# Expert ring of a two-block kernel: slots that hold half the rows of both experts, an earlier conditional, and banks written twice

## The reference, cut to what matters

```python
def hierarchical_moe(h, w_rg, b_rg, w_re, b_re, w1, w3, w2):
    # top-1 of 4 groups, top-2 of the 8 experts in it; 32 experts, D=1024, D_EXPERT=512
    ...
    e_w = jax.nn.softmax(e_val, axis=-1) * g_w
    ...
    def expert_block(args):
        xb, e = args
        hid = jax.nn.silu(xb @ w1[e]) * (xb @ w3[e])
        return hid @ w2[e]
    ys = lax.map(expert_block, (xs, blk_expert)).reshape(n_pad, D)
    ys = ys * wpad[:, None].astype(ys.dtype)
    out = jnp.zeros((T + 1, D), ys.dtype).at[tok].add(ys)[:T]
```

## Time and profile before

| | |
|---|---|
| median of 3 runs | 1216.96 us (1216.36 to 1217.27) |
| profiled execution | 1213.47 us, span 1211.6 us |
| mean granted TensorE clock | 0.985 |
| PE busy | 1145.1 us, 95% of the span |
| DVE, ACT, POOL busy | 40%, 34%, 19% |
| queue of the weight loads | 330.36 MB, 70.0% of 16 engines' span |
| chain that ended last | PE 71%, DMA 20%, DVE 5%, issue 1% |
| of it, loads of expert weights | 18% (`DMA ring<-in_w`) |
| of it, expert products | 12% L1144, 4% L1185 |
| loads of expert weights | 91 of 2048 KB, 17.5 us median to landing |

### The profile page before, as it was taken

One profiled execution on the slowest core, in us unless ns is written; L12 is line 12 of the kernel. 1 busy time (PEld: TensorE's weight loads), 2 busy tenths in 40 slices (PEclk: granted clock), 3 DMA queues, 4 the chain that ended last, 5 costly groups with the idle time before them and its releaser, 6 DMA issues.

```text
span 1211.6 us, 15514 instructions
## 1 busy us (share of the span) xinstructions
PE 1145.1 (95%) x5898; PEld 764.6 (63%) x5898; DVE 488.0 (40%) x967; ACT 409.8 (34%) x607; POOL 231.8 (19%) x104
## 2 busy tenths in 40 slices
PE   4899999989999999999999997999999999999998
PEld 1578767774444444444444445878877777888886
DVE  1595552762222222222222214589544643323226
ACT  3533444231111111111111115654345354434334
POOL 0362233200000000000000001410312435342522
PEclk8899999989999999999999998999999999999999
DMA  9886466678889999999999995443313455554541
GB/s 378 335 305 242 146 229 251 277 279 341 352 341 423 422 422 422 422 422 421 422 421 422 421 421 207 144 153 138 123 71 125 162 185 163 184 164 175 207 157 52
DMA packets 89191, 331.64 MB, mean 274 GB/s; under 512 B 3873, under 2 KB 26690, under 8 KB 62514
## 3 DMA queue, kind: packets, MB, share of 16 engines
q1 hardware_dynamic: 88512, 330.36, 70.0%
q0 software_dynamic: 432, 0.48, 0.2%
q10 hardware_dynamic: 194, 0.06, 0.0%
HBM read 329.84 MB, written 1.05 MB: 273 GB/s over the span
## 4 chain that ended last, share of the span: by engine, by line
PE 71%; DMA 20%; DVE 5%; issue 1%; SPq 1%; ACT 1%; POOL 0%; DVEq 0%; ACTq 0%
DMA ring<-in_w 18%; PE ps L831 14%; PE ps L832 13%; PE ps L833 13%; PE ps L1144 12%; PE ps L1185 4%; DMA ring<-in_w_ada 2%; PE ps L891 1%; PE ps L1116 1%; PE ps L1117 1%; PE ps L1287 1%; SPq L716 1%; PE ps L945 1%; PE ps L943 1%; PE ps L882 1%
## 5 line engine op out<-in xcount | busy, mean ns | idle before, releaser
L806 POOL TENSOR_TENSOR ring_r<-ring,ring_r 128x1024 fp32r<-128x1024 f32 x80 | 207.6, 2615 | 825.5 <-ACT ring_r L1486 825.5
L1144 PE MATMUL ps<-ring,arena 128*64 128x512 f32 x1008 | 228.5, 599 | 17.5 <-DMA ring<-in_w 17.5
L832 PE MATMUL ps<-ring_r,hl_r 128*128 128x512 f32 x528 | 210.7, 399 | 0.0
L831 PE MATMUL ps<-ring_r,hl_r 128*128 128x512 f32 x480 | 196.5, 409 | 9.1 <-DVE ring_r L1908 5.1
L833 PE MATMUL ps<-ring_r,hr_r 128*128 128x512 f32 x480 | 191.6, 399 | 0.0
L1486 ACT ACTIVATE ring_r<-ring 128x2048 fp32r<-128x2048 f32 x90 | 167.2, 1906 | 62.6 <-PE ps L833 45.0
L1144 PEld LDWEIGHTS ps<-ring,arena 128*64 128x64 f32 x1008 | 72.7, 138 | 154.0 <-issue 151.5
L1908 DVE TENSOR_TENSOR ring_r<-ring,ring_r 128x2048 fp32r<-128x2048 f32 x50 | 118.3, 2373 | 92.8 <-ACT ring_r L1486 92.6
L831 PEld LDWEIGHTS ps<-ring_r,hl_r 128*128 128x128 f32 x480 | 91.5, 191 | 37.3 <-issue 14.7
L832 PEld LDWEIGHTS ps<-ring_r,hl_r 128*128 128x128 f32 x528 | 100.6, 191 | 22.0
L833 PEld LDWEIGHTS ps<-ring_r,hr_r 128*128 128x128 f32 x480 | 91.3, 190 | 22.3
(11 more groups left out here) (363 smaller groups left out, 1656.6 us busy)
## 6 DMA issues: line engine op xcount, KB each, us to landing
ring<-in_w SPq DMA_DIRECT2D x91, 2048.0 KB, 17.5
ring<-in_w_in SPq DMA_DIRECT2D x21, 2048.0 KB, 8.8
ring<-in_w_ada SPq DMA_DIRECT2D x8, 2048.0 KB, 8.6
ring<-in_w_ffn_gate SPq DMA_DIRECT2D x11, 1024.0 KB, 5.3
ring<-in_w_ffn_up SPq DMA_DIRECT2D x11, 1024.0 KB, 8.0
ring<-in_w_ffn_down SPq DMA_DIRECT2D x5, 2048.0 KB, 7.8
ring<-in_w_ada SPq DMA_DIRECT2D x8, 1024.0 KB, 9.3
ring<-in_w_o SPq DMA_DIRECT2D x2, 2048.0 KB, 7.7
```

Source lines behind the costliest of these rows:

```text
L806: nc.gpsimd.tensor_tensor(rest[:, a:b], w[:, a:b], lead[:, a:b].bitcast(F32), ALU.subtract).then_inc(sem("w_rest_b"), 1)
L831: mm(o, lhsT=a_lead, rhs=b_lead, start=start, stop=False, skip_group_check=True)
L832: mm(o, lhsT=a_lead, rhs=b_rest, start=False, stop=False, skip_group_check=True)
L1144: last = mm(H[slots_of(e), :], lhsT=xs[:, k, slots_of(e)], rhs=w, start=k == 0, stop=k == KD - 1)
```

## The change

A ring slot now holds one half h of the rows (of w1, w3 or w2) of both experts of a pair. The product of a half can run when its slot has landed, and the slot is free at its end. `moe_w1_used` and `moe_w3_used` count halves, and ScalarE's and VectorE's waits on them are doubled. In w2 the order of the matmuls is half of the rows first, column half second. SyncE waits slot by slot. The early w1 load takes half 0 of both experts instead of all of one. `keep_x` writes all four banks before the rank matmuls, two of them again, and the other two again behind the rank. TensorE's conditional stands ahead of the last four pairs; these turns are written in both of its branches.

```diff
+LATE_TURNS = 4
-        MOE_USED = ("w1_used", "w1_used", "w3_used", "w3_used", "ys1_done", "ys1_done")
+        MOE_USED = ("w1_used", "w1_used", "w3_used", "w3_used", "ys0_done", "ys1_done")
...
+        def block_used(n, pairs):
+            return sem("moe_" + MOE_USED[n]), 2 * pairs - 1 + n % 2 if n < 4 else pairs
...
-            w = expert_w[n][bass.ds(2 * pair + n % 2, 1)]
-            view = ring[:, MOE_SLOT[n], :]
-            src = w.rearrange("e (h p j) n -> p (e h) (j n)", p=P, j=2 if n >= 4 else 4)
-            view = view.rearrange("p (h r) -> p h r", h=2)
+            w = expert_w[n][bass.ds(2 * pair, 2)]
+            view = ring[:, MOE_SLOT[n], :].rearrange("p (e r) -> p e r", e=2)
+            src = w.rearrange("e (h p j) n -> h p e (j n)", p=P, j=2 if n >= 4 else 4)[n % 2]
...
-            src = expert_w[0][2].rearrange("(h p j) n -> h p (j n)", p=P, j=4)
-            for h in range(2):
-                sp_.dma_start(early_w1[h], src[h]).then_inc(sem("early_w1_in"), 16)
+            for e in range(2):
+                src = expert_w[0][2 + e].rearrange("(h p j) n -> h p (j n)", p=P, j=4)
+                sp_.dma_start(early_w1[e], src[0]).then_inc(sem("early_w1_in"), 16)
...
-            sp_.wait_ge(sem("moe_w1_used"), 1)
-            expert_load(sp_, 1, 1, chunk_in)
-            expert_load(sp_, 0, 2, chunk_in)
-            sp_.wait_ge(sem("moe_w3_used"), 1)
-            expert_load(sp_, 2, 1, chunk_in)
-            expert_load(sp_, 3, 1, chunk_in)
+            for n, pair in ((0, 2), (1, 1), (2, 1), (3, 1)):
+                sp_.wait_ge(*block_used(n, 1))
+                expert_load(sp_, n, pair, chunk_in)
...
             with sp_.Fori(3, PAIRS) as i:
-                for n, name in enumerate(MOE_USED):
-                    sp_.wait_ge(sem("moe_" + name), i)
+                for n in range(6):
+                    sp_.wait_ge(*block_used(n, i))
                     expert_load(sp_, n, i, chunk_in)
...
-            for n in range(3):
+                into = dense.bank(f"moe{n}") if again else dense.claim(pe, f"moe{n}")
+                mm(into, lhsT=ident, rhs=x[:, t, h * COL:(h + 1) * COL], start=True, stop=True)
+
+            for n in range(4):
                 keep_x(n)
+            keep_x(0, True)
+            keep_x(1, True)
             o = small.claim(pe, "rank")
...
-            keep_x(3)
+            keep_x(2, True)
+            keep_x(3, True)
...
+                for h in range(2):
+                    if beside and h == 0:
+                        pe.wait_ge(sem("early_w1_in"), 32)
+                    else:
+                        chunk_ready(2 * n + h, i, done)
+                    if n == 0:
+                        pe.wait_ge(sem(f"moe_xs{h}_ready"), 4 * i + 4 * done + 4)
+                    for k in range(4 * h, 4 * h + 4):
+                        for e in range(2):
...
+                            last = mm(H[slots_of(e), :], lhsT=xs[:, k, slots_of(e)], rhs=w, start=k == 0, stop=k == KD - 1)
+                    last.then_inc(sem(("moe_w1_used", "moe_w3_used")[n]), 1)
...
-                for half, Y in enumerate((HA, HB)):
-                    for f in range(FT):
-                        for e in range(2):
+                for h in range(2):
+                    if not early:
+                        chunk_ready(4 + h, i, done)
+                    for half, Y in enumerate((HA, HB)):
+                        for f in (2 * h, 2 * h + 1):
+                            for e in range(2):
...
+                        if h == 1:
+                            last.then_inc(sem(f"moe_ys{half}_done"), 1)
...
-            with pe.Fori(3, PAIRS - 1) as i:
+            with pe.Fori(3, PAIRS - LATE_TURNS) as i:
                 turn(i, 0, 0)
-            last_turn(PAIRS - 1, 0, 0)
+            def late_turns():
+                with pe.Fori(PAIRS - LATE_TURNS, PAIRS - 1) as i:
+                    turn(i, 0, 0)
+                last_turn(PAIRS - 1, 0, 0)
             with pe.If(more > 0):
+                late_turns()
                 pe.wait_ge(sem("moe_ys_scaled"), 2 * PAIRS)
...
+            with pe.Else():
+                late_turns()
```

More of the change, by code:

```diff
@@ L556, in two_blocks @@
             landed[slot] += 16 * (PAIRS - len(BESIDE.get(n, ())))
-            busy[slot] = sem("moe_" + name), PAIRS
+            busy[slot] = sem("moe_" + name), 2 * PAIRS - 1 + n % 2 if n < 4 else PAIRS
         def in_ring(n, i):
@@ L752, in _ @@
             for n in (1, 2, 3):
-                sp_.wait_ge(sem("moe_" + MOE_USED[n]), 2)
+                sp_.wait_ge(*block_used(n, 2))
                 expert_load(sp_, n, 2, chunk_in)
@@ L768, in _ @@
                     e = sp_.snap(i % PAIRS)
-                    for n, name in enumerate(MOE_USED):
-                        sp_.wait_ge(sem("moe_" + name), i + PAIRS)
+                    for n in range(6):
+                        sp_.wait_ge(*block_used(n, i + PAIRS))
                         expert_load(sp_, n, e, spare_in)
@@ L1129, in up @@
             def up(n, H, i, done, beside=False):
[L1131 to L1145 removed]
+                for h in range(2):
[7 more added lines that the diff above has]
+                        for e in range(2):
+                            if beside and h == 0:
+                                w = early_w1[e][:, k * COL:(k + 1) * COL]
+                            else:
+                                w = wide(MOE_SLOT[2 * n + h])[:, 4 * e + k % 4, :]
+                            last = mm(H[slots_of(e), :], lhsT=xs[:, k, slots_of(e)], rhs=w, start=k == 0, stop=k == KD - 1)
+                    last.then_inc(sem(("moe_w1_used", "moe_w3_used")[n]), 1)
             def places(i, done, col0):
@@ L1159, in w2_rows @@
                     return early_w2[2 * e + f // 2][:, at % (2 * D):at % (2 * D) + COL]
-                return ring[:, MOE_SLOT[4 + e], at:at + COL]
+                at = (2 * e + f % 2) * D + half * COL
+                return ring[:, MOE_SLOT[4 + f // 2], at:at + COL]
             def middle(i, done, col0, more_pairs, early=0):
@@ L1177, in middle @@
                     pe.wait_ge(sem("early_w2_in"), 64 * early)
-                else:
-                    for e in range(2):
-                        chunk_ready(4 + e, i, done)
                 pe.wait_ge(sem("moe_hidT_ready"), i + done + 1)
-                for half, Y in enumerate((HA, HB)):
-                    for f in range(FT):
-                        for e in range(2):
-                            last = mm(Y[slots_of(e), :], lhsT=hidT[:, f, slots_of(e)],
-                                      rhs=w2_rows(e, f, half, early),
-                                      start=f == 0, stop=f == FT - 1)
-                    last.then_inc(sem(f"moe_ys{half}_done"), 1)
+                for h in range(2):
[4 more added lines that the diff above has]
+                            for e in range(2):
+                                last = mm(Y[slots_of(e), :], lhsT=hidT[:, f, slots_of(e)],
+                                          rhs=w2_rows(e, f, half, early),
+                                          start=f == 0, stop=f == FT - 1)
+                        if h == 1:
+                            last.then_inc(sem(f"moe_ys{half}_done"), 1)
             def combine(i, done):
```

26 lines of the change are left out of this document (5 added, 21 removed).

## The result

The changed kernel takes 1205.72 us (1203.98 to 1207.34) where the kernel before takes 1217.10. The ratio on record is 0.9912, 95% interval 0.9897 to 0.9927; the quotient of the two medians is 0.9907. Timed again on another chip it was 1206.88 against 1216.79, 0.9915 (0.9895 to 0.9936). The gain in the median is 9.9 to 11.4 us; 12.9 was predicted. The profiled execution took 1205.15 us, span 1203.3, and lies 8.3 us under the one of before (1213.47), which was itself 3.6 us under its median. Where these 3.6 us lie no trace shows, so what follows explains the 8.3.

The account below looks back on a forecast made before the run. The full queue of expert loads at 422 GB/s bounds the kernel. Earlier landing 6.7 + tail 7.0 - jump 0.8 = 12.9 us: profiled 1213.47 to 1200.6, median 1204.1; forecast's own range 1200 to 1208, with rivals (a), (b) 1198.5 to 1210.5.

Parts of the forecast that it names:

- Copies: Routing: six copies of x keep TensorE's clock up, so the first up projection ends 5.1 us earlier.
- rival (a): Routing: the clock still falls or the copies come too late; the 5.1 us go, 1209 us; chance 0.12.
- Slots at the front: Expert load queue: half-row slots fill holes, worth 1.6 to 2 us; with the copies, last landing 6.7 us earlier.
- The four holes that were left in the queue: Expert load queue: times still short of 422 GB/s at early w1, early w2, pair 3's first slot and its w2.
- Slots at the tail: Behind the last expert landing: only 3.5 us of w2 matmuls follow, so the last combine comes 3.0 us earlier.
- Conditional: Tail: jump moved ahead of pair 12; fq starts 12.0 us behind the landing, tail 7.0 us shorter, 3.0 from slots.
- The stall where it went: Jump at pair 12: TensorE 7.7 us late, 6.9 regained in later turns, 0.8 us left over.
- rival (b): New tail: clock falls in 2.5 us idle ahead of fq, costing 1.7 to 3.4 us, 1206 to 1207.5; chance 0.10.
- (c): Late loop: instructions missed again at two back edges and the exit, 16.5 us left over, 1220 us; chance 0.04.
- (d): Expert loads lose rate, stepping 2 MB between experts; slower than before, 1237 us at 387 GB/s; chance 0.05.
- (e): Expert load queue: holes stay and only the tail is gained, 6.2 us, 1211 us; chance 0.05.

Follow-up runs that it names:

- after2: The changed kernel, unchanged, timed and profiled again on another chip: 1206.88 us, ratio 0.9915 to the kernel before.
- after: The changed kernel itself, against the kernel before, in its first timing and profile: 1205.72 us, ratio 0.9912.
- u_cond: The changed kernel with TensorE's conditional put back behind the last pair: 1208.69 us, ratio 0.9941 to the kernel before.
- u_ring: The kernel before with the new copies of x and the early conditional, but without the half-row slots: 1210.39 us, ratio 0.9952 to the kernel before.
- empty_queue: The changed kernel with TensorE waiting for its own combine of pair 11 before the jump, so no matmul is queued: 1207.43 us, ratio 0.9920.
- warm_both_late2: The changed kernel with unused fill products in the last turn and ahead of fq and fk0, and two late turns instead of four: 1202.65 us, ratio 0.9886.
- fill_fk: The changed kernel with four unused 512-column products into fk0's free bank while TensorE waits for fk's weights: 1204.58 us, ratio 0.9895.
- warm_tail: The changed kernel with unused products filling TensorE's idle stretches in the last turn and ahead of fq: 1204.20 us, ratio 0.9889.
- late2: The changed kernel with two late turns instead of four, the jump standing ahead of pair 14: 1203.56 us, ratio 0.9888.
- nobranch: The changed kernel without TensorE's conditional and the further rounds, which this input doesn't take: 1202.21 us, ratio 0.9872.
- keep4: The changed kernel with four copies of x ahead of the rank matmuls instead of six, two again behind: 1204.12 us, ratio 0.9885.
- warm_both: The changed kernel with unused fill products in the last turn, ahead of fq and, four of them, ahead of fk0: 1201.20 us, ratio 0.9875.

## Why the prediction was right, and where not

The sign and the size came out: 9.9 to 11.4 us in the median instead of 12.9, within the forecast's own range. That the median came so close is partly luck: the sum was worked out on the profiled execution, and there the gain is 8.3. By its steps:

- **Copies: right, with a hole.** The front was to be 5.1 us earlier by them. Without a fall ahead of them it is 4.9 (after2: 20.0 to 15.1 behind the choice), in after's own execution 3.2 (20.0 to 16.9). The step that failed there is "six copies end at 261.1, so they are covered": it took 0.86 us a copy for granted. At 1.2 GHz they end at 264.2 and hold the rank matmuls up by 2.4 us, of which 1.7 are left at the end of the first w1 product. The text gave the price if the cover were gone, and rival (a) names copies that come too late, but neither says when that would be.
- **Slots at the front: right.** Predicted, with the copies, 6.7 us at the last landing. Measured 5.4 in after and 7.1 in after2; 5.9 to 7.1 in the seven others that have the slots and six copies and no fall inside the gather. The four holes that were left in the queue were forecast at 3.0, 1.2, 6.4 and 2.6 us and are 3.0, 1.5, 6.7 and 2.5 in after2. What was off is the split: the forecast gave the slots 1.6 by themselves and the clock 5.1, and alone they give 1.3 and 3.6; the rest comes only with both.
- **Slots at the tail: right.** 3.0 predicted, 3.2 measured (u_cond) and 3.0 (15.24 in u_ring to 12.2).
- **Conditional: right in sum.** The tail was to shrink by 7.0 and does by 7.5 where the clock held in the last w2 and TensorE wasn't late for it (12.2), 6.3 in after. What is late next was named rightly, ScalarE's split of fq and then the rows.
- **The stall where it went: over-priced.** The term was 5.24 + 2.5 us late at pair 12, 6.9 regained, 0.8 left. It is 1.83 late, and nothing is left in after's profile. The failed step is to move the 5.24 from a place with an empty queue to one with a full one. (The terms regained add up to 7.0, not 6.9.) Where TensorE was late by more, in empty_queue and warm_both_late2, 1.2 and 0.5 us are left at fq, so setting lateness against slack, as the forecast did, was right in kind.
- **The clock behind the tail: missed in the sum.** It was rival (b), at 1.7 to 3.4 us, with a chance of 0.10. It happened, 1.2 us in w2 and 1.6 in fq, and once more where it wasn't looked for, 1.1 at fk; 0.85 us went at the load of wo's weights, for which no cause is shown. That is 4.8 us in after, 3.6 of them behind fq's start. The rival was under-weighted though its own numbers had it: 2.5 us of idle were forecast ahead of fq, 2.34 came, and the earlier trace rows show a fall behind 3.4 us of idle, with light matmuls round it. Adding up: 12.9 + 0.5 (tail) + 0.8 (jump) + 0.3 (ahead of the choice) - 1.3 (front) - 4.8 = 8.4, where the two profiled spans differ by 8.3.

Rivals (c), (d) and (e) are out: one "issue" gap, 422 GB/s, and holes filled. Of (a) the clock in the gather held in after and after2 and fell in fill_fk; the late copies came in after.

**Open.** Why the load of wo's weights takes longer in some kernels (0 to 1.2 us) isn't settled: it happens with falls of the clock (after, after2, u_ring, empty_queue) and without (fill_fk). Medians and profiled executions of one kernel differ by up to 5 us (warm_tail), and the medians of late2, nobranch, keep4 and warm_tail aren't told apart. What the jump costs in the median stays open: nobranch is clear of after and of empty_queue, which speaks for a cost that the profiles don't show, but keep4 has the jump too and lies only 1.9 us above nobranch on the same chip. That the clock's falls are what warm_both gained rests on three profiles with 463.9 us behind fq (warm_tail, warm_both, warm_both_late2) against 465.1 to 467.9 in the ten others of the changed kind; the kernel before, with falls at 740.8 and 788.5, has 464.06 too.

## What to carry to other kernels

Price a jump by what is queued on the engine when it comes: with matmuls queued the array stood for 1.8 us here, with none for 5.2 to 6.2. Leave it enough turns to be made good, a fall of the clock behind it included. When a change shortens a stage, look at what the shorter stage leaves TensorE to do: behind a wait of 2.3 us ahead of fq the clock fell in seven profiles of nine. A few products into a free bank took that away in three profiles of three and delayed nothing (12.21 us to fq in warm_both); a gain in the median is shown for warm_both, 5.7 us under after2. Buffers that come free earlier and a consumer that starts earlier were worth more together, up to 7.1 us, than the sum of each alone, 4.9, since each alone left another hole in the queue of transfers.

## What the runs showed of the hardware

- A jump over some hundreds of instructions took 5.2 to 6.2 us of TensorE with nothing queued (before, u_cond, empty_queue), and 1.76 to 1.91 with matmuls queued (ten profiles, at pair 12 or 14).
- The clock fell to 1.2 GHz while TensorE was busy, among matmuls of 36 columns (255.0 in after, not in after2) and inside a gather of 128 columns (271.0 in fill_fk, idle for 0.54 us in the 6.5 before).
- Behind the same wait of 2.31 to 2.34 us ahead of fq the clock fell for 3.4 us in seven profiles and held in two (empty_queue, fill_fk).
- A step of 2 MB in HBM between the two runs of one slot's load cost nothing here at 8 KB a run: 422 GB/s as with the 1 MB step of before.
